# Two expert tables laid side by side: one 8 KB gather per expert instead of two of 4 KB, and weights made in two parts per block

## The chip, the cores and the metric

One NeuronCore of one Trainium2 chip runs the whole program. The metric is the device time of that core in microseconds (us); the time before is the median of three runs, and everything else is read from one profiled execution of the same kernel.

## What is computed

The reference is one inference step of a two-layer network over 384 tokens of width 1024 (128 context tokens and 256 noisy ones), float32 throughout. Layer 0 mixes the tokens with an RG-LRU, layer 1 with gated linear attention (GLA); after each mixer comes a PEER channel mixer, which is where the change lies. Its core, from the reference:

```python
cand = (v1[..., :, None] + v2[..., None, :]).reshape(T, PEER_HEADS, -1)
sc, pos = lax.top_k(cand, PEER_TOPK)
eid = jnp.take_along_axis(cid, pos, axis=-1)
gate = jax.nn.softmax(sc, axis=-1)
...
ub = jnp.take(u_tab, eb, axis=0)
act = jax.nn.gelu(jnp.einsum('td,thkd->thk', xb, ub).astype(jnp.float32))
vb = jnp.take(v_tab, eb, axis=0)
return jnp.einsum('thk,thkd->td', (gb * act).astype(vb.dtype), vb)
```

So each token picks 16 experts for each of 8 heads. For every expert a row u of 1024 floats (4 KB) is dotted with the token, the result goes through a gelu and is multiplied by the gate, and the row v of the same expert (another 4 KB) is added to the token's output with that weight. Each table has 16,384 rows a layer. 384 x 8 x 16 experts at 8 KB are 402.7 MB a layer.

## The kernel before

The tokens lie in three tiles of 128 (one token to a partition). A **block** is one head of one tile: 24 blocks a layer (`NB`), in the order of `h, t = divmod(b, NT)`, 16 experts (`TOPK`) each, and n numbers the experts through both layers. Each expert of a block is one indirect gather of 128 rows, one row to a partition.

There is no scheduler: every engine runs its own list of instructions, and semaphores join them. Ring buffers set how far one may run ahead of another.

- **GpSimd (POOL)**, `gathers` (lines 302 to 323): for each block it waits for the indices (`idx_ready`), issues the 16 u gathers (L314) into a ring of `US` = 8 buffers, then the 16 v gathers (L321) into a ring of `VS` = 16. A u buffer is free when VectorE has dotted it (`u_free`), a v buffer when TensorE has used it (`v_free`). The rings are 4 KB slices of `arena`, 24 in all.
- **VectorE (DVE)**, `peer` (lines 1068 to 1109): 16 dot products (L1085, in place, `accum_out` keeps the sum), the inner polynomial of the gelu (L1089 to L1091), softmax and dot folded into `ex` (L1095 to L1098), the top 16 of the keys' scores for two blocks ahead (`row_tops`, L1101), the weights (L1105) once ScalarE has the tanh, and then the choice of the experts for two blocks ahead (`choose`, which ends with `idx_ready` at L1053).
- **ScalarE (ACT)**, `peer` (lines 416 to 476): when a head begins it first copies the queries (L421, waits for TensorE), then the tanh (L458), then for each expert a 128 x 128 diagonal matrix of the weights (L467, a ring of `DS` = 8); ahead of expert 8 of a head's first block it copies the scores (L430).
- **TensorE (PE)**, `peer` (lines 714 to 728): for each expert two matmuls (L725) of the diagonal with the two halves of the v row, summed in PSUM; each is two passes in the records, so 4 records an expert. A head's first block begins with the next head's queries (L689), and ahead of expert 8 stand its scores (L698).
- **SyncE (SP)**: streams weights. In PEER it reloads `wq_slab` (1 MB, L264 and L267) for each head when the queries of the one before are done; behind the last one in layer 0 it loads the first four 1 MB slabs of GLA's input weights (`stream`, L257), whose buffers lie idle by then.

In both layers the last block is cut into parts of 8, 4 and 4 experts (`LAST_PARTS`), so that the end of a layer has little left to do; every other block is one part of 16. After layer 0 come the residual and norm, the small projections of GLA, and its large projections, which read the slabs (L651).

```python
mm = pe.matmul(acc[t][:, half * 512:(half + 1) * 512], diag[j % DS][:, :],
               vbuf[n % VS][:, half * 512:(half + 1) * 512], start=False, stop=True,
               skip_group_check=True)
```

Of the kernel before, what the change touches and what calls it, by code (L numbers as in the profile page):

```python
# [17 lines left out]
NT = T // P  # L18
# [5 lines left out]
SLABS = 4  # L24
# [74 lines left out]
def build(nc, x_t, pos_t, vecs, ident_d, mask_d, iota_d, keys_t, ada_w, peer_wq, peer_u, peer_v, rg_w_in,  # L99
          rg_wa, rg_wi, rg_w_out, gla_w_in, w_alpha, state_gla, gla_w_out, y_t, st_rg, st_gla):  # L100
    ctx = ExitStack()
    with ctx:
# [73 lines left out]
        ubuf = [arena[:, i * D:(i + 1) * D] for i in range(US)]  # L176
        vbuf = [arena[:, (US + i) * D:(US + i + 1) * D] for i in range(VS)]
# [53 lines left out]
        def _(sp):  # L231
# [65 lines left out]
        def _(pool):  # L297
# [1051 lines left out]
```

## Time and profile before

| what | value |
|---|---|
| median of 3 runs | 2669.35 us (2669.15 to 2673.39) |
| span of the profiled execution | 2672.5 us |
| TensorE busy, VectorE, ScalarE, GpSimd | 79%, 60%, 19%, 57% |
| software DMA queue (the gathers) | 805.4 MB, 76.4% of 16 engines' span |
| layer 0 PEER, first gather issued to last matmul | 280.64 to 1328.58 us |
| layer 1 PEER, the same | 1616.14 to 2650.42 us |

The profiler gives the profiled execution only as its span, first to last instruction; it is 3.2 us above the median and inside 0.9 us of the slowest of the three runs. The busy shares are means over stages: the two PEER stages make up 2082 us of the span, and the rest (RG-LRU, GLA, head and tail of the program) has other limits and is not touched, but for four slab loads. A profile row names the line, the engine, the operation and the buffers; idle time stands before an instruction with what ended it.

### The profile page before, as it was taken

The numbers are of one execution on the slowest core, as the hardware profiler recorded it, in microseconds if no ns is written. First come the engines' busy times: TensorE is split into PE (matmuls) and PEld (weight loads), VectorE is DVE, ScalarE is ACT, GpSimd is POOL, SyncE is SP. The second block draws the span as 40 slices with busy tenths as digits, with TensorE's granted clock in tenths as the row PEclk, the third lists the DMA queues.
The fourth block names the chain that finished last, engine by engine and source line by source line (L and its number), as shares of the span: only waits on it lengthen the run. The fifth ranks groups of instructions, "written<-read, shape, count | busy, mean of one in ns | idle before, by whom it ended". The sixth has DMA issues, their size and how long they took to land.

```text
span 2672.5 us, 20762 instructions
## 1 busy us (share of the span) xinstructions
PE 2123.0 (79%) x6324; PEld 1045.4 (39%) x6324; DVE 1597.3 (60%) x3961; ACT 498.2 (19%) x1291; POOL 1528.1 (57%) x1543
## 2 busy tenths in 40 slices
PE   6998678696968685976989996786969687788777
PEld 2555433242424332432447654342424243333333
DVE  3244666757576666767432436667576666767655
ACT  2251211111111111111242112110111111111112
POOL 0000577777777767777500005777777777777773
PEclk9999799898989797988989998898989898989989
DMA  9992699999999999999723117999999999999996
GB/s 295 317 327 95 243 410 407 406 404 405 400 399 407 409 401 399 394 410 409 308 68 95 60 36 262 405 400 409 406 406 404 396 407 409 404 407 394 409 409 242
DMA packets 326365, 913.32 MB, mean 342 GB/s; under 512 B 31952, under 2 KB 128464, under 8 KB 325744
## 3 DMA queue, kind: packets, MB, share of 16 engines
q0 software_dynamic: 221184, 805.40, 76.4%
q1 hardware_dynamic: 97840, 101.20, 11.8%
q10 hardware_dynamic: 7232, 5.39, 0.7%
q8 instruction: 52, 0.85, 0.1%
q14 instruction: 57, 0.47, 0.0%
HBM read 909.26 MB, written 2.63 MB: 341 GB/s over the span
## 4 chain that ended last, share of the span: by engine, by line
PE 22%; POOL 10%; DMA 9%; DVE 4%; issue 4%; ACT 1%; DVEq 0%; ACTq 0%; POOLq 0%
PE psum L725 11%; DMA arena<-in_peer_u,idx 9%; POOL arena L314 7%; PE psum L651 5%; POOL arena L321 3%; PE psum L689 2%; PE psum L827 2%; DVE arena L1085 1%; PE psum L905 1%; PE psum L880 1%; PE psum L638 0%; PE psum L809 0%; ACT diag L467 0%; DVE i12u L1020 0%; ACT arena L377 0%
## 5 line engine op out<-in xcount | busy, mean ns | idle before, releaser
L725 PE MATMUL psum<-arena,diag 128*128 128x512 f32 x3072 | 1413.2, 622 | 464.7 <-ACT diag L467 464.5
L1085 DVE SCALAR_TENSOR_TENSOR arena<-arena,xtok 128x1024 f32<-128x1024 f32 x768 | 939.6, 1225 | 639.7 <-DMA arena<-in_peer_u,idx 611.2
L314 POOL DMA_INDIRECT arena<-in_peer_u,idx x768 | 778.9, 1014 | 874.1 <-issue 523.3
L725 PEld LDWEIGHTS psum<-arena,diag 128*128 128x128 f32 x3072 | 608.5, 200 | 1257.4 <-issue 1257.4
L321 POOL DMA_INDIRECT arena<-in_peer_v,idx x768 | 745.2, 970 | 234.2 <-issue 211.6
L467 ACT ACTIVATE diag<-ident,wts 128x128 f32<-128x128 f32 x768 | 259.3, 393 | 475.1 <-PE psum L725 370.0
L651 PE MATMUL psum<-arena,slab 128*128 128x384 f32 x672 | 227.7, 497 | 7.3 <-DVE arena L1154 5.1
L689 PE MATMUL psum<-area 128*128 128x384 f32 (+1 forms) x512 | 165.2, 482 | 8.3 <-DMA area<-in_peer_wq 8.3
L651 PEld LDWEIGHTS psum<-arena,slab 128*128 128x128 f32 x672 | 128.2, 193 | 101.3 <-issue 13.0
L458 ACT ACTIVATE tanh<-inner 128x16 f32<-128x16 f32 (+2 forms) x52 | 11.1, 213 | 760.7 <-DVE inner L1091 760.7
L689 PEld LDWEIGHTS psum<-area 128*128 128x128 f32 x512 | 99.0, 194 | 76.0 <-DMA area<-in_peer_wq 10.9
L421 ACT ACTIVATE area<-psum 128x384 f32<-128x384 f32 (+1 forms) x32 | 15.3, 477 | 314.8 <-PE psum L689 314.8
L616 PE MATMUL psum<-slab,cond 128*2 128x256 f32 x528 | 53.1, 409 | 21.3 <-DMA slab<-in_ada_w 21.3
L1085 DVE DVE_READ_ACCUMULATOR arena<-arena,xtok 128x1 f32 x768 | 63.0, 82 | 0.0
L827 PE MATMUL psum<-slab,arena 128*128 128x256 f32 x192 | 41.6, 379 | 0.0
L362 ACT ACTIVATE arena<-xT 128x384 f32<-128x384 f32 x40 | 20.1, 520 | 101.8 <-DVE xT L1163 46.7
L1196 DVE COPY arena<-psum 128x256 f32<-128x256 f32 x12 | 5.1, 424 | 56.1 <-PE psum L827 56.1
L827 PEld LDWEIGHTS psum<-slab,arena 128*128 128x128 f32 x192 | 36.5, 190 | 5.2
L616 PEld LDWEIGHTS psum<-slab,cond 128*2 128x2 f32 x528 | 19.2, 89 | 47.9 <-DMA slab<-in_ada_w 27.9
L1045 DVE TENSOR_TENSOR small<-ab,iota 128x512 f32<-128x512 f32 x48 | 35.7, 743 | 0.0
L1048 DVE TENSOR_TENSOR small<-small,i 128x512 f32<-128x512 f32 x48 | 33.2, 692 | 1.7
L1049 DVE TENSOR_REDUCE e<-small 128x32 f32<-128x512 f32 x48 | 32.9, 686 | 1.6
(218 smaller groups left out, 1329.1 us busy)
## 6 DMA issues: line engine op xcount, KB each, us to landing
slab<-in_ada_w SPq DMA_DIRECT2D x33, 1024.0 KB, 8.3
area<-in_peer_wq SPq DMA_DIRECT2D x16, 1024.0 KB, 16.4
arena<-in_peer_u,idx POOLq DMA_INDIRECT x768, 8.1
arena<-in_peer_v,idx POOLq DMA_INDIRECT x768, 7.9
slab<-in_gla_w_in SPq DMA_DIRECT2D x12, 1024.0 KB, 5.6
keys<-in_ada_w SPq DMA_DIRECT2D x8, 1024.0 KB, 9.1
area<-in_ada_w SPq DMA_DIRECT2D x7, 1024.0 KB, 7.9
slab<-in_rg_w_in SPq DMA_DIRECT2D x5, 1024.0 KB, 11.7
```

Source lines behind the costliest of these rows:

```text
L314: pool.indirect_dma_start(ubuf[n % US], None, u_rows, bass.IndirectOffsetOnAxis(ap=rows[:, j:j + 1], axis=0)).then_inc(u_in[n % US], 16)
L321: pool.indirect_dma_start(vbuf[n % VS], None, v_rows, bass.IndirectOffsetOnAxis(ap=rows[:, j:j + 1], axis=0)).then_inc(v_in[n % VS], 16)
L467: act.activation(diag[j % DS][:, :], ident[:, :], ACT.Copy, scale=wts[t][:, j:j + 1]).then_inc(sem("diag_ready"), 1)
L616: mm = pe.matmul(out[32 * s:32 * s + 2, o:o + SW], cond[:, c, :], slab[SLOT[k]][:, c, :], start=False, stop=(c == C - 1), skip_group_check ...
L651: mm = pe.matmul(out, slab[SLOT[k]][:, c, (n % 2) * P:(n % 2 + 1) * P], rhs[:, c, :], start=(c == 0), stop=(c == C - 1))
L689: mm = pe.matmul(bank[6 + half][:, t0 * P:T], wq_slab[:, c, half * P:(half + 1) * P], hP[:, c, t0 * P:T], start=(c == 0), stop=(c == C - 1))
L725: mm = pe.matmul(acc[t][:, half * 512:(half + 1) * 512], diag[j % DS][:, :], vbuf[n % VS][:, half * 512:(half + 1) * 512], start=False, st ...
L827: mm = pe.matmul(bank[(2 + i) % 4][:, 0:SW], hT[:, c, t * P:(t + 1) * P], slab[SLOT[k]][:, c, :], start=(c == 0), stop=(c == C - 1))
L1045: link(dve.tensor_tensor(oh, ab[:, :, :].unsqueeze(3).to_broadcast([P, 2, TOPK, TOPK]), iota16[:, :].unsqueeze(1).unsqueeze(1).to_broadcas ...
L1048: link(dve.tensor_tensor(oh, oh, i12[:, :, :].unsqueeze(2).to_broadcast([P, 2, TOPK, TOPK]), ALU.mult))
L1049: link(dve.tensor_reduce(e12[:, :, :], oh, AX_X, ALU.add))
L1085: dve.scalar_tensor_tensor(ubuf[n % US], ubuf[n % US], 1.0, xtok[:, t * D:(t + 1) * D], ALU.mult, ALU.mult, accum_out=dots[t][:, j:j + 1]) ...
```

## The change

On the host the tables u and v are joined along their last axis, so one table `peer_uv` has rows of 8 KB with u in front. One gather brings an expert's whole row into one of `RS` = 16 buffers of 8 KB. Twelve of them lie in `arena`, four are the weight slabs; so SP may load GLA's first slabs only when the last row of layer 0 is used (a new wait). The dots are written into the first half of the row, TensorE reads the second half, and the buffer is free when TensorE has used it. Every block but the last is cut into two parts of 8 experts, each with its own inner, tanh and weights; `row_tops` stays in the first part, `choose` behind the last.

```diff
-US, VS, DS = 8, 16, 8
+RS, DS = 16, 8
+PARTS = (range(0, 8), range(8, 16))
...
-NSTEP = NB - 1 + len(LAST_PARTS)
+NSTEP = 2 * (NB - 1) + len(LAST_PARTS)
...
-        ubuf = [arena[:, i * D:(i + 1) * D] for i in range(US)]
-        vbuf = [arena[:, (US + i) * D:(US + i + 1) * D] for i in range(VS)]
+        row = [arena[:, 2 * i * D:2 * (i + 1) * D] for i in range(RS - SLABS)]
+        row += [s[:, :, :].rearrange("p c n -> p (c n)") for s in slab[0:SLABS]]
...
-            return LAST_PARTS if b == NB - 1 else (range(TOPK),)
+            return LAST_PARTS if b == NB - 1 else PARTS
...
             sp.dma_start(st_rg, rgfin[:, :, :]).then_inc(sem("st_rg_out"), 16)
+            sp.wait_ge(row_free, NB * TOPK)
             stream(PLACE["gla_in", 0], len(SEQ))
...
-                    for part in parts(b):
-                        for j in part:
-                            n = (layer * NB + b) * TOPK + j
-                            if n >= US:
-                                pool.wait_ge(u_free, n - US + 1)
-                            pool.indirect_dma_start(
-                                ubuf[n % US], None, u_rows,
-                                bass.IndirectOffsetOnAxis(ap=rows[:, j:j + 1], axis=0)).then_inc(u_in[n % US], 16)
-                        for j in part:
-                            n = (layer * NB + b) * TOPK + j
-                            if n >= VS:
-                                pool.wait_ge(v_free, n - VS + 1)
-                            pool.indirect_dma_start(
-                                vbuf[n % VS], None, v_rows,
-                                bass.IndirectOffsetOnAxis(ap=rows[:, j:j + 1], axis=0)).then_inc(v_in[n % VS], 16)
+                    for j in range(TOPK):
+                        n = (layer * NB + b) * TOPK + j
+                        if n >= RS:
+                            pool.wait_ge(row_free, n - RS + 1)
+                        pool.indirect_dma_start(
+                            row[n % RS], None, rows_of,
+                            bass.IndirectOffsetOnAxis(ap=rows[:, j:j + 1], axis=0)).then_inc(row_in[n % RS], 16)
...
-                                           vbuf[n % VS][:, half * 512:(half + 1) * 512], start=False, stop=True,
+                                           row[n % RS][:, D + half * 512:D + (half + 1) * 512], start=False, stop=True,
...
-                            dve.wait_ge(u_in[n % US], 16 * (n // US + 1))
-                            dve.scalar_tensor_tensor(ubuf[n % US], ubuf[n % US], 1.0, xtok[:, t * D:(t + 1) * D],
+                            dve.wait_ge(row_in[n % RS], 16 * (n // RS + 1))
+                            dve.scalar_tensor_tensor(row[n % RS][:, 0:D], row[n % RS][:, 0:D], 1.0,
+                                                     xtok[:, t * D:(t + 1) * D],
...
-                        if ahead < NB:
+                        if ahead < NB and i == 0:
                             dve.wait_ge(sem("s_ev"), 2 * (PH * layer + ahead // NT + 1))
                             row_tops(ahead)
...
-                        if layer * NB + b >= 3:
-                            dve.wait_ge(v_free, (layer * NB + b - 2) * TOPK)
+                        if i == 0 and layer * NB + b >= 3:
+                            dve.wait_ge(row_free, (layer * NB + b - 2) * TOPK)
...
-        "ada_w": a["ada_w"], "peer_wq": a["peer_wq"], "peer_u": a["peer_u"], "peer_v": a["peer_v"],
+        "ada_w": a["ada_w"], "peer_wq": a["peer_wq"],
+        "peer_uv": np.concatenate([a["peer_u"], a["peer_v"]], axis=2),
```

## Rows read from the trace of the kernel before

**Rows 1.** Page of the profile: span, busy time by engine, DMA rate in 40 slices.

```profile
span 2672.5 us, 20762 instructions
...
PE 2123.0 (79%) x6324; PEld 1045.4 (39%) x6324; DVE 1597.3 (60%) x3961; ACT 498.2 (19%) x1291; POOL 1528.1 (57%) x1543
...
GB/s 295 317 327 95 243 410 407 406 404 405 400 399 407 409 401 399 394 410 409 308 68 95 60 36 262 405 400 409 406 406 404 396 407 409 404 407 394 409 409 242
```

**Rows 2.** Chain that ended last, share of the span by line.

```profile
PE psum L725 11%; DMA arena<-in_peer_u,idx 9%; POOL arena L314 7%; PE psum L651 5%; POOL arena L321 3%; PE psum L689 2%; PE psum L827 2%; DVE arena L1085 1%; PE psum L905 1%; PE psum L880 1%; PE psum L638 0%; PE psum L809 0%; ACT diag L467 0%; DVE i12u L1020 0%; ACT arena L377 0%
```

**Rows 3.** Stretches in PEER: busy us (x instructions) by engine, PE clock, DMA share, GB/s.

```profile
360.00:380.00 20.00, 11.38 (x23) 5.12 (x24) 13.26 (x51) 4.67 (x14) 15.22 (x16) 0.74 1.03 410
1620.00:1640.00 20.00, 14.23 (x40) 7.73 (x39) 16.30 (x51) 3.23 (x8) 10.20 (x10) 0.74 0.84 292
1660.00:2620.00 960.00, 748.90 (x1756) 339.27 (x1756) 642.98 (x1649) 148.90 (x465) 717.35 (x730) 0.90 1.02 405
```

**Rows 4.** Page: software DMA queue; issues of the u gathers with median landing time.

```profile
q0 software_dynamic: 221184, 805.40, 76.4%
...
arena<-in_peer_u,idx POOLq DMA_INDIRECT x768, 8.1
```

**Rows 5.** Stretches ahead of PEER, where weights arrive; columns as in rows 3.

```profile
80.00:120.00 40.00, 37.96 (x222) 19.87 (x217) 9.39 (x16) 9.58 (x20) 0.00 (x0) 1.00 1.04 332
160.00:200.00 40.00, 38.62 (x226) 20.84 (x224) 18.46 (x23) 12.71 (x19) 0.00 (x0) 1.00 1.06 338
```

**Rows 6.** Timeline of POOL, both layers: start, duration, [idle before].

```profile
280.64 1.08 POOL L314 DMA_INDIRECT arena<-in_peer_u,idx  x1 [276.11 <-DVE flag L1053]
...
1616.14 0.94 POOL L314 DMA_INDIRECT arena<-in_peer_u,idx  x1 [301.05 <-issue]
...
1636.35 1.97 POOL L314 DMA_INDIRECT arena<-in_peer_u,idx  x1 [0.30 <-issue]
```

**Rows 7.** Timeline, the last four experts of each layer.

```profile
1319.78 8.80 PE L725 MATMUL psum<-arena,diag 128*128 128x512 f32 x16 [3.13 <-ACT diag L467]
...
2635.79 1.12 POOL L321 DMA_INDIRECT arena<-in_peer_v,idx  x1 [0.30 <-issue]
...
2638.72 1.22 DVE L1085 SCALAR_TENSOR_TENSOR arena<-arena,xtok 128x1024 f32<-128x1024 f32 x1
...
2641.62 8.80 PE L725 MATMUL psum<-arena,diag 128*128 128x512 f32 x16 [3.13 <-ACT diag L467]
```

**Rows 8.** Timeline of one block: DVE, then PE.

```profile
701.82 0.17 DVE L1089 TENSOR_TENSOR inner<-dots 128x16 f32<-128x16 f32 x1
...
705.47 0.17 DVE L1105 SCALAR_TENSOR_TENSOR wts<-tanh,ex 128x16 f32<-128x16 f32 x1
...
711.54 0.06 DVE L1053 MEMSET flag<- 128x1 f32 x1
...
720.03 1.50 PE L698 MATMUL psum<-keys,area 128*128 128x128 f32 x12
...
722.49 13.97 PE L725 MATMUL psum<-arena,diag 128*128 128x512 f32 x32 [0.96 <-ACT diag L467]
```

**Rows 9.** Chain in order of time: queries of one head on PE.

```profile
2028.62 10.34 PE psum L689 x32
```

**Rows 10.** Stretches of 2 us around an idle time of PE; columns as in rows 3.

```profile
1260.00:1262.00 2.00, 0.00 (x0) 0.00 (x0) 1.93 (x5) 0.00 (x0) 1.39 (x3) 0.50 1.02 406
1266.00:1268.00 2.00, 2.00 (x3) 0.67 (x2) 0.00 (x0) 0.40 (x1) 1.39 (x3) 0.50 1.06 418
1270.00:1272.00 2.00, 2.00 (x6) 0.90 (x5) 0.00 (x0) 0.40 (x1) 1.39 (x3) 1.00 1.03 412
```

**Rows 11.** Page: the dot products of DVE.

```profile
L1085 DVE SCALAR_TENSOR_TENSOR arena<-arena,xtok 128x1024 f32<-128x1024 f32 x768 | 939.6, 1225 | 639.7 <-DMA arena<-in_peer_u,idx 611.2
```

**Rows 12.** Timeline: SP's four slabs for GLA, and PE's first matmuls on them.

```profile
961.21 38.66 SPq L257 DMA_DIRECT2D slab<-in_gla_w_in  x4
...
1362.55 2.29 PE L651 MATMUL psum<-arena,slab 128*128 128x384 f32 x3
```

More of the change, by code:

```diff
@@ L96, in __call__, with build @@
         self.need(self.mark(ins))
-def build(nc, x_t, pos_t, vecs, ident_d, mask_d, iota_d, keys_t, ada_w, peer_wq, peer_u, peer_v, rg_w_in,
+def build(nc, x_t, pos_t, vecs, ident_d, mask_d, iota_d, keys_t, ada_w, peer_wq, peer_uv, rg_w_in,
           rg_wa, rg_wi, rg_w_out, gla_w_in, w_alpha, state_gla, gla_w_out, y_t, st_rg, st_gla):
@@ L212, in build @@
         slab_in = [sem(f"slab_in{i}") for i in range(SLABS + 2)]
-        u_in = [sem(f"u_in{i}") for i in range(US)]
-        v_in = [sem(f"v_in{i}") for i in range(VS)]
-        u_free, v_free = sem("u_free"), sem("v_free")
+        row_in = [sem(f"row_in{i}") for i in range(RS)]
+        u_used, row_free = sem("u_used"), sem("row_free")
         (vec_in, const_in, x_in, pos_in, bd_in, gla_small_in, mask_in, s0_in) = (
@@ L302, in gathers @@
             def gathers(layer):
-                u_rows = peer_u.rearrange("l n d -> (l n) d")
-                v_rows = peer_v.rearrange("l n d -> (l n) d")
+                rows_of = peer_uv.rearrange("l n d -> (l n) d")
                 pool.wait_ge(sem("h_ready"), 32 * (layer + 1))
@@ L439, in total @@
                 def total(t):
-                    act.wait_ge(v_free, (layer * NB + NB - NT + t + 1) * TOPK)
+                    act.wait_ge(row_free, (layer * NB + NB - NT + t + 1) * TOPK)
                     act.activation(xtok[:, t * D:(t + 1) * D], acc[t], ACT.Copy).then_inc(sem("acc_ev"), 1)
@@ L456, in peer @@
                         p = slice(part[0], part[-1] + 1)
-                        act.wait_ge(sem("inner_ready"), layer * NSTEP + b + i + 1)
+                        act.wait_ge(sem("inner_ready"), layer * NSTEP + 2 * b + i + 1)
                         act.activation(tanh[t][:, p], inner[t][:, p], ACT.Tanh, scale=GELU_C
                                        ).then_inc(sem("tanh_ready"), 1)
-                        act.wait_ge(sem("w_ready"), layer * NSTEP + b + i + 1)
+                        act.wait_ge(sem("w_ready"), layer * NSTEP + 2 * b + i + 1)
                         for j in part:
@@ L465, in peer @@
                             if n >= DS:
-                                act.wait_ge(v_free, n - DS + 1)
+                                act.wait_ge(row_free, n - DS + 1)
                             act.activation(diag[j % DS][:, :], ident[:, :], ACT.Copy,
@@ L721, in peer @@
                         n = (layer * NB + b) * TOPK + j
-                        pe.wait_ge(v_in[n % VS], 16 * (n // VS + 1))
+                        pe.wait_ge(row_in[n % RS], 16 * (n // RS + 1))
                         pe.wait_ge(sem("diag_ready"), n + 1)
@@ L725, in peer @@
                             mm = pe.matmul(acc[t][:, half * 512:(half + 1) * 512], diag[j % DS][:, :],
-                                           vbuf[n % VS][:, half * 512:(half + 1) * 512], start=False, stop=True,
+                                           row[n % RS][:, D + half * 512:D + (half + 1) * 512], start=False, stop=True,
                                            skip_group_check=True)
-                        mm.then_inc(v_free, 1)
+                        mm.then_inc(row_free, 1)
                 pe.wait_ge(sem("acc_ev"), NT * (layer + 1))
@@ L1050, in choose @@
                 if b >= 4:
-                    dve.wait_ge(v_free, (layer * NB + b - 3) * TOPK)
+                    dve.wait_ge(row_free, (layer * NB + b - 3) * TOPK)
                 link(dve.scalar_tensor_tensor(idx[q][:, :], e12[:, 0, :], float(NK), e12[:, 1, :], ALU.mult, ALU.add))
@@ L1083, in peer @@
                             n = (layer * NB + b) * TOPK + j
-                            dve.wait_ge(u_in[n % US], 16 * (n // US + 1))
-                            dve.scalar_tensor_tensor(ubuf[n % US], ubuf[n % US], 1.0, xtok[:, t * D:(t + 1) * D],
+                            dve.wait_ge(row_in[n % RS], 16 * (n // RS + 1))
+                            dve.scalar_tensor_tensor(row[n % RS][:, 0:D], row[n % RS][:, 0:D], 1.0,
+                                                     xtok[:, t * D:(t + 1) * D],
                                                      ALU.mult, ALU.mult, accum_out=dots[t][:, j:j + 1]
-                                                     ).then_inc(u_free, 1)
-                        dve.wait_ge(u_free, (layer * NB + b) * TOPK + part[-1] + 1)
+                                                     ).then_inc(u_used, 1)
+                        dve.wait_ge(u_used, (layer * NB + b) * TOPK + part[-1] + 1)
                         link(dve.tensor_tensor(inner[t][:, p], dots[t][:, p], dots[t][:, p], ALU.mult))
@@ L1098, in peer @@
                         link(dve.tensor_tensor(ex[q][:, p], ex[q][:, p], dots[t][:, p], ALU.mult))
-                        if ahead < NB:
+                        if ahead < NB and i == 0:
                             dve.wait_ge(sem("s_ev"), 2 * (PH * layer + ahead // NT + 1))
                             row_tops(ahead)
-                        dve.wait_ge(sem("tanh_ready"), layer * NSTEP + b + i + 1)
-                        if layer * NB + b >= 3:
-                            dve.wait_ge(v_free, (layer * NB + b - 2) * TOPK)
+                        dve.wait_ge(sem("tanh_ready"), layer * NSTEP + 2 * b + i + 1)
+                        if i == 0 and layer * NB + b >= 3:
+                            dve.wait_ge(row_free, (layer * NB + b - 2) * TOPK)
                         dve.scalar_tensor_tensor(wts[t][:, p], tanh[t][:, p], 1.0, ex[q][:, p], ALU.add, ALU.mult
```

## Prediction

> **What bounds the kernel now.** I began with the page: no engine is busy throughout (PE 79%, DVE 60%), but in 28 of the 40 slices the transfer rate stands at 394 to 410 GB/s [rows 1]. The chain that ended last agrees: it wanders between the u gathers' DMA, POOL issuing them and PE's L725 [rows 2], which is what a ring looks like when a transfer is at its bottom. Then the stretches. In the quiet middle of PEER the 16 DMA engines are full (share 1.03) and move 410 GB/s, and the best slices of the page have 409 and 410 [rows 1, 3]; I take 409.5; over 960 us of layer 1 the mean is 405; only at a layer's start is it low, 292 GB/s in 20 us [rows 3]. A u gather lands 8.1 us after its issue, although it needs only 1.28 us of the engines (0.524 MB at 409.5 GB/s), so several stand in the queue [rows 4]: in PEER the kernel waits for DMA throughput, not for latency or for an engine.
>
> The two PEER stages, from first gather issued to last matmul, take 1047.9 us (280.64 to 1328.58) and 1034.3 us (1616.14 to 2650.42) [rows 6, 7]. The change can win only there.
>
> **Part 1: bigger packets.** The bytes stay: 384 gathers of 8 KB rows replace 768 of 4 KB ones a layer. What can change is the cost of a packet. Ahead of PEER, where weights arrive in 1 KB runs, the engines are just as full (share 1.04 and 1.06) but move 332 and 338 GB/s [rows 5]. With 16 engines a 1 KB packet at 335 takes 48.9 ns, a 4 KB packet at 409.5 takes 160.0 ns. The line through both has 0.03617 ns per byte and 11.9 ns per packet. So an 8 KB packet is estimated at 160.0 + 4096 x 0.03617 = 308.1 ns instead of 320.0, and a gather (8 packets per engine) at 2.465 us instead of 2 x 1.280 = 2.560 (425 GB/s). No gather with 8 KB rows is in the trace, so the price is bounded: 2.560 if a row is cut into two packets or the packet cost is none of this kind; 2.370 if the packet cost vanished altogether. I take 2.465, since it extends two measured points by one doubling. Over 768 gathers the step from 2.560 to 2.465 is worth 73 us.
>
> The Trainium skill ("DMA: Bandwidth & Descriptors", section "Why small descriptors are slow (HBM only)") puts the fixed cost at about 3 cycles a packet beside 128 beats for 4 KB; by that the saving would be about 1.1%, some 23 us instead of 73, and the result near 2608. The rows' 11.9 ns of 160.0 speak for more than that.
>
> **Part 2: the layer's start.** Today POOL issues 8 u gathers and then stands until DVE, still choosing the experts of block 1, frees a buffer; then each issue lasts 1.97 us instead of 0.94 while DVE's dots run back to back, plus 0.30 between them [rows 6]. That is the hole of 292 GB/s [rows 3]: (409.5 - 292)/409.5 x 20 = 5.7 us in those 20 us, about 9 in all with the 20 after. With 16 rows of 1 MB the queue holds 16 x 2.465 = 39 us of work at once. At that ring's first turn I expect a short gap, because block 0's first row can't be freed before PE has done the queries of head 1, whose weights now share the engines with a full queue: I put it at 3 us, beside 2 us from issue to full rate.
>
> **Part 3: the wait on SP.** The four GLA slabs, now issued at 961.2 us into the full queue [rows 12], move behind layer 0. A 1 MB weight load costs 64 x 48.9 ns = 3.13 us of the engines, so PEER of layer 0 loses 12.5 us of transfers. Behind the last row they need about 13 us; PE reads the first 34 us after its last L725 (1328.6 to 1362.55) [rows 7, 12]. Nothing else is queued on SP but the later slabs, which follow one another at once. Cost 0; if the cover were gone it would be at most 13 us.
>
> **Part 4: the layer's end.** Today the last v row lands at about 2641, and PE runs its last four experts from 2641.62 for 8.80 us: 9.1 us behind the landing [rows 7]. Now u arrives with v, so behind the last landing come a dot, the inner steps, tanh and weights: 2.90 us from the start of the last dot (2638.72) to PE, then 8.80. The end is 11.7 us behind the landing, 2.6 more a layer.
>
> **Part 5: instructions.** 384 gathers fewer on POOL a layer: it is not the bound, and is hidden by DMA now. Two parts add to 23 blocks three inner steps, one `ex` and one `wts` on DVE (0.17 us each [rows 8]) and one tanh: DVE's block is 16 x 1.23 for the dots [rows 11], 3.65 for inner, tops and weights (701.82 to 705.47), 6.1 for `choose` (to 711.54) [rows 8], plus 1.2: 31 us under 39.4 of DMA. Hidden, and if not, under 1 us a block.
>
> **The sum** for layer 1: 2 + 3 + 384 x 2.465 (946.6) + 7 weight loads x 3.13 (21.9) + 11.7 = 985.2, against 1034.3: 49.1 won. Layer 0 loses the slabs too and should take the same 985.2, against 1047.9: 62.7. Together 111.8 us from 2672.5 in the profiled execution; that lies 3.2 above the median, so the forecast is 2669.35 - 111.8 = 2557.5, **about 2558 us**. (A check of the method: for layer 1 before it gives 2 + 983.0 + 21.9 + 9.1 = 1016; the missing 18 us are the 9 of the start and 9 of slices under 409.)
>
> **What comes next: PE and the ring.** A row's buffer is now held until PE is done with it, through the landing of the 7 rows behind it. PE needs 13.97 us for 8 experts at full clock, 1.50 for scores [rows 8], 10.34 for queries [rows 9]. After an idle stretch the granted clock is 0.50 (1.2 GHz), and it stayed there some 6 us into the next work before it was 1.00 (2.4 GHz) [rows 10]; that costs 3 us a part. A head is 6 x 13.97 + 11.8 + 6 x 3 = 114 us of PE in 3 x 39.4 + 3.1 = 121 of DMA: it fits, but barely. The tight spot is a head's first block. If the block before lands at 0, PE starts its last part at 3, ends at 20 (cold), queries until 30.4, ACT copies them only then and makes the tanh that stood behind, PE frees the new block's first row at about 34, and the gather for it can start at 36. The queue runs dry at 39.4 to 42.5. Margin 3 to 6 us.
>
> **The rivals.**
> - **Cut packets, 2630 us.** The 8 KB row moves as two 4 KB packets, or costs as much. Each layer is 2 + 3 + 983.0 + 21.9 + 11.7 = 1021.6: 12.7 and 26.3 won, 39 in all. For it: no packet of this queue above 4 KB is in the trace, so nothing shows that it makes them. Against it: nothing in the trace either. The Trainium skill (same page, section "SWDGE vs HWDGE vs iDMA") says a packet of the software path is preferably at most 4096 B, which would give this case; no row here shows it.
> - **PE late at each head, slower: about 2716 us.** If the clock stays low through the queries (10.34 more) and 3 us longer in each of the two parts beside them, PE is 16.3 us late. Less the margin of 5, that is 11.3 us in 14 heads, 158 us on 2558. It decides from about 13 us a head. Against it: queries now follow directly behind 8 experts, so PE is at work before them; today at 2028.62 they took 10.34, full clock.
> - **POOL becomes the bound, slower: near 3100.** If POOL's time for a gather grows with its bytes, it is 2 x 1.97 + 0.30 = 4.24 us beside back-to-back dots, for half of the rows, against 2.24 for the others: mean 3.24 x 384 = 1244 a layer. Against it: the number of rows, 128, stays.
> - **No saving of any kind, 2669:** the new holds eat what the start and slabs give.
> - **Packets free of cost, 2485:** 2.370 a gather, 73 us less than forecast.
>
> **Chances.** Forecast 0.58, cut packets 0.25, PE late 0.06, POOL 0.03, no saving 0.04, free packets 0.04. The likeliest case alone reaches from 2535 (2.435 a gather) to 2608 (2.53); with the second case and 12 us for a gap at each turn the range is 2525 to 2650, which leaves out 0.17. About 0.2% is what a measurement of this kernel can tell from no change. Faster by more than that: 0.58 + 0.25 + 0.04 and part of the doubtful cases, 0.89; within 0.03; slower 0.08.
>
> **What would show it.** DMA rate in the middle of PEER at 420 to 428 GB/s (410: cut packets, and twice the packets per gather). No hole in the first 40 us. POOL busy about halved, at 0.94 to 1.1 us a gather. Layers of about 985 us. L651 not waiting for a slab. PE's share up, with queries still at 10.3. Wrong if the DMA share falls below 1.0 at the first block of each head, or POOL's mean is near 2 us.

## The result and the profile after

| | median | runs |
|---|---|---|
| before | 2671.37 us | 2669.15 to 2674.18, 4 runs |
| after | 2607.26 us | 2606.61 to 2611.63, 4 runs |

The ratio is 0.9765 with an interval of 0.9751 to 0.9778: 64 us are won (2671.37 - 2607.26), where the prediction said 112. The direction is the one forecast, and 2607 is inside the range of 2525 to 2650; what is to be explained is the 47 us that are missing.

The page of the kernel after, its lines that answer to [rows 1, 2, 4]: span, busy time, rate in 40 slices, two DMA queues, the chain by line, two groups of instructions, and two landing times.

```profile
span 2604.7 us, 20351 instructions
...
PE 2125.3 (82%) x6324; PEld 1044.5 (40%) x6324; DVE 1598.7 (61%) x4191; ACT 486.4 (19%) x1337; POOL 948.2 (36%) x775
...
GB/s 303 318 328 112 276 406 419 420 418 421 417 417 418 410 418 412 408 420 419 268 73 98 61 37 294 421 418 421 418 421 418 421 418 413 418 409 415 417 421 184
...
q0 software_dynamic: 110592, 805.36, 74.7%
q1 hardware_dynamic: 97840, 101.20, 12.1%
...
DMA slab<-in_peer_uv,idx 28%; PE psum L717 24%; PE psum L643 8%; DMA arena<-in_peer_uv,idx 8%; POOL slab L313 3%; POOL arena L313 2%; DMA slab<-in_ada_w 2%; DMA area<-in_peer_wq 2%; PE psum L681 2%; PE psum L819 2%; PE psum L608 2%; DVE slab L1077 2%; PE psum L897 1%; PE psum L758 1%; ACT diag L459 1%
...
L717 PE MATMUL psum<-arena,diag 128*128 128x512 f32 x2304 | 1087.6, 632 | 368.6 <-ACT diag L459 368.6
L313 POOL DMA_INDIRECT arena<-in_peer_uv,idx x576 | 698.9, 1213 | 1530.7 <-PE psum L717 879.6
...
area<-in_peer_wq SPq DMA_DIRECT2D x16, 1024.0 KB, 25.4
...
arena<-in_peer_uv,idx POOLq DMA_INDIRECT x576, 17.1
```

POOL fell from 57% to 36%. The rate in PEER's slices went from 394 to 410 up to 408 to 421, not to 425. The gathers' queue has 110,592 packets for the same 805 MB, half of the 221,184 in [rows 4], so a row of 8 KB does go as one packet (98,304 of the packets are rows; the other 12,288 are 16 of 4 B for each gather). The chain is now landings of rows (28% + 8%) and PE's L717. POOL stands 879.6 us behind PE's L717, which is only the ring being full.

Stretches of the kernel after; columns as in [rows 3]. The last line is the kernel before, in the same 20 us of layer 0.

```profile
300.00:320.00 20.00, 9.24 (x22) 5.27 (x23) 7.88 (x30) 0.49 (x1) 1.66 (x1) 0.62 1.02 418
324.00:326.00 2.00, 0.90 (x2) 0.49 (x3) 1.65 (x4) 1.70 (x7) 0.00 (x0) 1.00 0.45 113
340.00:360.00 20.00, 16.68 (x42) 7.36 (x41) 16.26 (x47) 6.10 (x21) 10.67 (x9) 1.00 1.01 423
1240.00:1260.00 20.00, 16.35 (x33) 6.82 (x33) 10.92 (x23) 3.43 (x11) 8.76 (x8) 0.84 1.01 421
1268.00:1270.00 2.00, 2.00 (x6) 0.95 (x5) 1.25 (x3) 1.28 (x4) 0.00 (x0) 1.00 0.26 107
1270.00:1272.00 2.00, 2.00 (x6) 0.81 (x5) 1.23 (x2) 0.00 (x0) 0.00 (x0) 1.00 0.07 29
1640.00:2560.00 920.00, 738.91 (x1712) 331.46 (x1711) 641.71 (x1751) 139.36 (x476) 438.43 (x360) 0.92 1.01 418
...
300.00:320.00 20.00, 11.88 (x32) 6.49 (x30) 14.42 (x26) 0.98 (x2) 16.45 (x12) 0.84 0.83 263
```

In the quiet middle the engines are full and move 421 to 423 GB/s, over 920 us 418. The hole at the layer's start is gone (418 in 300:320, against 263 before), and a short one at 324 to 330 took its place. At the layer's end (1268 on) the share drops to 0.07, about one engine of 16, while rows still land.

DVE's dot products, each with its idle time and what ended it; the first is row 32 of layer 0, the last is row 384.

```profile
371.96 1.25 DVE L1077 SCALAR_TENSOR_TENSOR slab<-slab,xtok 128x1024 f32<-128x1024 f32 x1 [1.25 <-DMA slab<-in_peer_uv,idx]
...
1240.80 1.23 DVE L1077 SCALAR_TENSOR_TENSOR arena<-arena,xtok 128x1024 f32<-128x1024 f32 x1 [1.25 <-DMA arena<-in_peer_uv,idx]
...
1243.29 1.22 DVE L1077 SCALAR_TENSOR_TENSOR arena<-arena,xtok 128x1024 f32<-128x1024 f32 x1 [1.25 <-DMA arena<-in_peer_uv,idx]
...
1245.78 1.23 DVE L1077 SCALAR_TENSOR_TENSOR arena<-arena,xtok 128x1024 f32<-128x1024 f32 x1 [1.26 <-DMA arena<-in_peer_uv,idx]
...
1275.53 1.23 DVE L1077 SCALAR_TENSOR_TENSOR slab<-slab,xtok 128x1024 f32<-128x1024 f32 x1 [1.22 <-DMA slab<-in_peer_uv,idx]
```

In the middle each dot waits 1.25 us for its row, and they begin 2.49 us apart: the starts of the dots show when the rows land. Layer 0's PEER went from 1047.9 us to 1010.5 (first gather issued at 278.75, last matmul ended at 1282.25 + 7.03 = 1289.28), layer 1's from 1034.3 to 1006.8. The sum had 985.2 for both, so 25.3 and 21.6 us of the 47 are here.

### The profile page after: what moved, and what is told of

Its sections match the earlier page's. It is cut to its first block, busy times and chain, and to the rows that moved or that the text cites. A ratio compares the mean times of both kernels' runs of the same rounds, so it can differ in the third digit from the quotient of the medians.

```text
span 2604.7 us, 20351 instructions
## 1 busy us (share of the span) xinstructions
PE 2125.3 (82%) x6324; PEld 1044.5 (40%) x6324; DVE 1598.7 (61%) x4191; ACT 486.4 (19%) x1337; POOL 948.2 (36%) x775
## 3 DMA queue, kind: packets, MB, share of 16 engines
q0 software_dynamic: 110592, 805.36, 74.7%
q1 hardware_dynamic: 97840, 101.20, 12.1%
## 4 chain that ended last, share of the span: by engine, by line
PE 42%; DMA 41%; DVE 6%; POOL 5%; issue 3%; ACT 2%; SPq 0%; DVEq 0%; ACTq 0%
DMA slab<-in_peer_uv,idx 28%; PE psum L717 24%; PE psum L643 8%; DMA arena<-in_peer_uv,idx 8%; POOL slab L313 3%; POOL arena L313 2%; DMA slab<-in_ada_w 2%; DMA area<-in_peer_wq 2%; PE psum L681 2%; PE psum L819 2%; PE psum L608 2%; DVE slab L1077 2%; PE psum L897 1%; PE psum L758 1%; ACT diag L459 1%
## 5 line engine op out<-in xcount | busy, mean ns | idle before, releaser
L717 PE MATMUL psum<-arena,diag 128*128 128x512 f32 x2304 | 1087.6, 632 | 368.6 <-ACT diag L459 368.6
L313 POOL DMA_INDIRECT arena<-in_peer_uv,idx x576 | 698.9, 1213 | 1530.7 <-PE psum L717 879.6
L717 PEld LDWEIGHTS psum<-arena,diag 128*128 128x128 f32 x2304 | 459.9, 203 | 984.4 <-issue 984.4
L1077 DVE SCALAR_TENSOR_TENSOR arena<-arena,xtok 128x1024 f32<-128x1024 f32 x576 | 687.0, 1223 | 268.4 <-DMA arena<-in_peer_uv,idx 262.7
L1077 DVE SCALAR_TENSOR_TENSOR slab<-slab,xtok 128x1024 f32<-128x1024 f32 x192 | 235.4, 1228 | 227.4 <-DMA slab<-in_peer_uv,idx 227.4
L717 PE MATMUL psum<-slab,diag 128*128 128x512 f32 x768 | 337.4, 593 | 0.0
L313 POOL DMA_INDIRECT slab<-in_peer_uv,idx x192 | 245.3, 1278 | 71.5 <-issue 39.3
L459 ACT ACTIVATE diag<-ident,wts 128x128 f32<-128x128 f32 x768 | 235.0, 389 | 107.8 <-DVE wts L1098 107.4
L643 PE MATMUL psum<-arena,slab 128*128 128x384 f32 x672 | 227.8, 497 | 7.1 <-DVE arena L1147 4.9
L450 ACT ACTIVATE tanh<-inner 128x8 f32<-128x8 f32 (+1 forms) x98 | 20.3, 207 | 1140.5 <-DVE inner L1084 1140.5
L717 PEld LDWEIGHTS psum<-slab,diag 128*128 128x128 f32 x768 | 146.2, 190 | 183.4 <-issue 183.4
L681 PE MATMUL psum<-area 128*128 128x384 f32 (+1 forms) x512 | 165.6, 483 | 35.0 <-DMA area<-in_peer_wq 35.0
L643 PEld LDWEIGHTS psum<-arena,slab 128*128 128x128 f32 x672 | 128.6, 194 | 100.7 <-issue 12.8
L681 PEld LDWEIGHTS psum<-area 128*128 128x128 f32 x512 | 99.4, 195 | 102.7 <-DMA area<-in_peer_wq 37.7
L1098 DVE SCALAR_TENSOR_TENSOR wts<-tanh,ex 128x8 f32<-128x8 f32 (+1 forms) x98 | 16.4, 167 | 81.6 <-issue 52.6
## 6 DMA issues: line engine op xcount, KB each, us to landing
area<-in_peer_wq SPq DMA_DIRECT2D x16, 1024.0 KB, 25.4
slab<-in_rg_w_in SPq DMA_DIRECT2D x5, 1024.0 KB, 11.7
```

The costliest lines, as they stand in the source:

```text
L313: pool.indirect_dma_start(row[n % RS], None, rows_of, bass.IndirectOffsetOnAxis(ap=rows[:, j:j + 1], axis=0)).then_inc(row_in[n % RS], 16)
L450: act.activation(tanh[t][:, p], inner[t][:, p], ACT.Tanh, scale=GELU_C).then_inc(sem("tanh_ready"), 1)
L459: act.activation(diag[j % DS][:, :], ident[:, :], ACT.Copy, scale=wts[t][:, j:j + 1]).then_inc(sem("diag_ready"), 1)
L643: mm = pe.matmul(out, slab[SLOT[k]][:, c, (n % 2) * P:(n % 2 + 1) * P], rhs[:, c, :], start=(c == 0), stop=(c == C - 1))
L681: mm = pe.matmul(bank[6 + half][:, t0 * P:T], wq_slab[:, c, half * P:(half + 1) * P], hP[:, c, t0 * P:T], start=(c == 0), stop=(c == C - 1))
L1077: dve.scalar_tensor_tensor(row[n % RS][:, 0:D], row[n % RS][:, 0:D], 1.0, xtok[:, t * D:(t + 1) * D], ALU.mult, ALU.mult, accum_out=dots[t ...
```

## The experiments

All times are medians beside runs of the kernel before on the same chip; those medians were 2669.9 to 2672.5.

**E1: the same ring and parts, but two gathers of 4 KB a row.**

```diff
-pool.indirect_dma_start(row[n % RS], None, rows_of, ...).then_inc(row_in[n % RS], 16)
+for k, table in enumerate((peer_u, peer_v)):
+    pool.indirect_dma_start(row[n % RS][:, k * D:(k + 1) * D], None, table.rearrange("l n d -> (l n) d"),
+                            ...).then_inc(row_in[n % RS], 16)
-dve.wait_ge(row_in[n % RS], 16 * (n // RS + 1))
+dve.wait_ge(row_in[n % RS], 32 * (n // RS + 1))
```

> The changed kernel (2607 us) with each row fetched by two gathers of 4 KB from the two old tables into the two halves of the same buffer: ring, parts and slab wait as changed, only packet size and number of gathers as before. If the saving per packet is what pays (2.49 us a row after, 2.56 before), the time rises by 768 x 0.07 = 54 us to about 2661, the rate in the middle of PEER falls to 409 to 410 GB/s at a DMA share of 1.03. If ring, start and slabs give all of the gain, it stays at 2607. If POOL can't issue two gathers a row in the time (2 x 1.24 us alone, up to 2 x 2.27 beside the dots), it goes above 2680 with a DMA share under 1.

Measured: 2749.25 us (2745.02 to 2751.57), ratio 1.0297 (1.0280 to 1.0314). The chain from the page, and the stretch 1680 to 2680:

```profile
POOL arena L313 23%; PE psum L717 17%; POOL slab L313 9%; PE psum L643 7%; DMA slab<-in_peer_v,idx 7%; DMA arena<-in_peer_v,idx 3%; PE psum L681 3%; DMA slab<-in_ada_w 2%; PE psum L608 2%; PE psum L819 2%; DVE slab L1077 1%; DMA area<-in_peer_wq 1%; PE psum L897 1%; PE psum L758 1%; ACT diag L459 1%
...
1680.00:2680.00 1000.00, 769.41 (x1730) 343.54 (x1731) 648.28 (x1771) 141.39 (x482) 780.22 (x721) 0.89 1.00 385
```

POOL's own instructions are now 32% of the chain, and the rate is 385 over a thousand microseconds. An issue takes 0.94 us, but up to 1.99 beside DVE's dots, plus 0.30 between two: in the thousand microseconds that is 780 + 721 x 0.30 = 996 us of POOL, so with two gathers a row POOL is the limit. So the packet's price can't be read here, and another thing can: without the joined table, this ring and these parts are 3% slower than the kernel before. In the kernel before, a u issue took 1014 ns in the mean and a v issue 970; here they take 1107 and 1057 (buffers in `arena`). POOL was near its limit there too: 717 + 730 x 0.30 = 936 of 960 us [rows 3].

**E2: the kernel before, with the slab loads behind the last row.**

```diff
+            sp.wait_ge(v_free, NB * TOPK)
             stream(PLACE["gla_in", 0], len(SEQ))
```

> The kernel before with only the new wait of SP ahead of GLA's first slabs. If the 4 MB they bring are 4 x 3.13 us of full DMA engines in PEER and free behind it, the time falls by 12.5 us to about 2659. If the transfers were hidden already, or if the slabs come late for L651, it stays at 2671 or rises by up to 13 us.

Measured: 2658.63 us (2655.29 to 2662.00), ratio 0.9955 (0.9938 to 0.9972): 11.8 us less. In the trace PEER of layer 0 takes 1035.6 us instead of 1047.9, and layer 1's first gather comes 285.4 us behind its end, where it was 287.6. Part 3 stands: 4 MB of weights out of the full queue are worth 12 us and cost nothing behind it.

**E3: E2 with a u ring of 16, eight of its buffers in the slabs.**

```diff
-US, VS, DS = 8, 16, 8
+US, VS, DS = 16, 16, 8
-        ubuf = [arena[:, i * D:(i + 1) * D] for i in range(US)]
+        ubuf = [arena[:, i * D:(i + 1) * D] for i in range(8)]
+        ubuf += [s[:, 4 * k:4 * k + 4, :].rearrange("p c n -> p (c n)") for s in slab[0:SLABS] for k in range(2)]
```

> The kernel before with that wait and a u ring of 16 buffers of 4 KB (8 of them in the slabs), still two gathers of 4 KB. If the hole at each layer's start came from the u ring of 8, 9 us a layer go beside the 12.5 of the slabs: 2671 - 12.5 - 18 = about 2641. If the start is limited otherwise (POOL at 2.27 us a gather beside the dots), it equals the run with the wait alone, 2659.

Measured: 2649.38 us (2648.51 to 2654.06), ratio 0.9930 (0.9914 to 0.9947): 9.3 less than E2, half of the 18. Layer 1 begins at another time in each run, so the stretches are those from 4 us behind its first gather: E2 (first gather at 1600.04), then E3 (1596.03).

```profile
1604.00:1624.00 20.00, 18.04 (x42) 9.22 (x41) 15.69 (x49) 3.24 (x8) 10.12 (x8) 0.66 0.80 275
...
1600.00:1620.00 20.00, 17.16 (x41) 8.71 (x40) 15.68 (x49) 3.23 (x8) 16.03 (x14) 0.66 1.00 368
1620.00:1640.00 20.00, 12.31 (x30) 6.18 (x29) 19.51 (x61) 3.64 (x11) 16.34 (x13) 0.83 0.98 355
```

The deeper ring takes about half of the start's hole. What is left is POOL's issue at its slower pace: 16.03 + 14 x 0.30 fill the first 20 us, and two gathers a row keep that.

**E4: the kernel after, dots over 128 of 1024 columns.** It leaves out 7/8 of each dot product, so its output is another one.

```diff
-dve.scalar_tensor_tensor(row[n % RS][:, 0:D], row[n % RS][:, 0:D], 1.0, xtok[:, t * D:(t + 1) * D], ...
+dve.scalar_tensor_tensor(row[n % RS][:, 0:P], row[n % RS][:, 0:P], 1.0, xtok[:, t * D:t * D + P], ...
```

> The changed kernel with dots over 128 of the 1024 columns; it leaves out 7/8 of each dot product, so the weights are other numbers. DVE's time for a row falls from 1.23 to about 0.2 us. If the DMA engines alone set 2.49 us a row, the rate in the middle stays 421 GB/s and the time falls by only 2 to 4 us (the last dots). If DVE's dots beside POOL's descriptors or the SBUF traffic of the dots slow the transfers, the rate rises to 425 or more and the time falls by 8 us or more.

Measured: 2603.71 us (2603.43 to 2603.96), ratio 0.9754 (0.9737 to 0.9770): 3.5 less than the kernel after. Its stretch of 920 us:

```profile
1640.00:2560.00 920.00, 745.65 (x1706) 333.21 (x1705) 310.01 (x1749) 139.81 (x477) 338.88 (x357) 0.91 1.01 417
```

DVE's work is halved (310 us against 642) and the rate is the same: neither DVE nor POOL beside it holds up the kernel after. What is left is DMA, whose engines are full (share 1.01). The 3.5 us are within what was said for the dots that stand on the path at both ends of a layer.

**E5: E1 and E4 together**, which differs from E4 by the packet's size and the number of gathers alone (it leaves out the same 7/8 of the dots).

> Two gathers of 4 KB a row into the same ring, and dots over 128 of the 1024 columns (7/8 of each dot product is left out), so that DVE no longer stretches POOL's gathers: POOL then needs 2 x 1.24 = 2.49 us a row, less than 2.56. If a 4 KB packet itself costs more, the rate in the middle is 409 to 410 GB/s at a DMA share of 1.03 and the time is 2604 + 768 x 0.07 = about 2658. If packet size is worth nothing and the 2749 us of the two gathers with full dots was POOL alone, the rate is 421 and the time about 2604 to 2610.

Measured: 2657.41 us (2654.72 to 2658.86), ratio 0.9945 (0.9930 to 0.9960). Its dots, and its stretch of 920 us:

```profile
1710.32 0.29 DVE L1077 SCALAR_TENSOR_TENSOR arena<-arena,xtok 128x128 f32<-128x128 f32 x1 [2.22 <-DMA arena<-in_peer_v,idx]
...
1712.88 0.29 DVE L1077 SCALAR_TENSOR_TENSOR arena<-arena,xtok 128x128 f32<-128x128 f32 x1 [2.26 <-DMA arena<-in_peer_v,idx]
...
1640.00:2560.00 920.00, 732.60 (x1684) 328.91 (x1684) 311.23 (x1731) 136.02 (x465) 664.67 (x699) 0.91 1.03 407
```

With the short dots POOL has time over, if little (665 + 699 x 0.30 = 874 of 920 us), the engines are full at share 1.03, and rows land 2.56 us apart. The difference to E4, 53.7 us over 768 rows, is 0.070 us a row: the price of 16 packets of 4 KB and two gathers against 8 of 8 KB and one, on each engine. Part 1 had 0.095 (73 us). The medians of before beside E4 and E5 differ by 0.5 us.

**E6: the kernel after, weights laid on the host so that a slab is one 8 KB run a partition.**

```diff
-src = peer_wq[layer].rearrange("(c p) n -> p c n", p=P)
-sp.dma_start(wq_slab, src[:, :, 0:SW]).then_inc(wq_in, 16)
+src = peer_wq[layer]
+sp.dma_start(wq_slab, src[0]).then_inc(wq_in, 16)
...
+    def slabs(w):
+        return w.reshape(w.shape[0], C, P, -1, SW).transpose(0, 3, 2, 1, 4)
```

> The changed kernel with all weight slabs laid on the host so that each slab is one run of 8 KB a partition instead of eight of 1 KB; same bytes, same order. If a packet costs 11 to 12 ns beside its bytes, a 1 MB slab takes 2.49 us of full engines instead of 3.13: 14 loads in PEER give 9 us, and of the 57 ahead of layer 0's PEER (36 us of engine time) the part on the chain, 10 to 25 us: 2570 to 2590 in all, with the rate ahead of PEER above 380 GB/s where the engines are full. If the size of the packet matters only on the gathers' software queue, it stays at 2607 and 332 to 338 GB/s.

Measured: 2593.68 us (2592.14 to 2597.71), ratio 0.9708 (0.9693 to 0.9723): 13.6 less than the kernel after, and outside the 2570 to 2590 expected. Page lines, and a stretch ahead of PEER:

```profile
q1 hardware_dynamic: 15408, 101.20, 10.1%
...
area<-in_peer_wq SPq DMA_DIRECT2D x16, 1024.0 KB, 9.3
...
80.00:120.00 40.00, 38.98 (x265) 21.09 (x254) 11.44 (x20) 8.75 (x19) 0.00 (x0) 1.00 0.89 340
```

Packets of the weights' queue fell from 97,840 to 15,408, and `wq_slab` lands 9.3 us after its issue, not 25.4. In the trace the two PEER stages are 6.4 and 3.0 us shorter (1004.1 and 1003.8), the 9 us expected of the 14 loads. The missing part is the one ahead of PEER: the rate per full share rose (340 at 0.89 is 382; in [rows 5] it is 319), but the engines now stand idle for a tenth of that time, and the first gather is issued at 280.80, no sooner than the 278.75 of the kernel after. Ahead of PEER the engines were not what the time hung on.

**E7: the kernel after, last block in four parts of 4.**

```diff
-LAST_PARTS = (range(0, 8), range(8, 12), range(12, 16))
+LAST_PARTS = (range(0, 4), range(4, 8), range(8, 12), range(12, 16))
```

> The changed kernel with the last block of each layer in four parts of 4. If PE's 16 experts in one go (30.4 us from the weights of the first 8) set the end of a layer, PE begins 10 us earlier and the end is set by the last landing: 3 us a layer less, about 2601. If the last landing sets it already, it stays at 2607.

Measured: 2603.93 us (2599.52 to 2605.04), ratio 0.9745 (0.9731 to 0.9758), 3.3 less than the kernel after; the two intervals overlap. The last dot of layer 0 and PE behind it, then PE at the end of layer 1:

```profile
1278.29 1.23 DVE L1077 SCALAR_TENSOR_TENSOR slab<-slab,xtok 128x1024 f32<-128x1024 f32 x1 [1.23 <-DMA slab<-in_peer_uv,idx]
...
1281.20 7.11 PE L717 MATMUL psum<-slab,diag 128*128 128x512 f32 x16 [2.74 <-ACT diag L459]
...
2573.51 8.59 PE L717 MATMUL psum<-slab,diag 128*128 128x512 f32 x16 [3.01 <-ACT diag L459]
```

PE had done all earlier experts and stood 2.74 us when the last weights came: the end is 10.0 us behind the last dot's start (1288.31 - 1278.29), against 13.75 in the kernel after. In layer 1 PE was done too and stood 3.01 us, but its last four experts took 8.59 us instead of 7.03: the end is 11.5 us behind the last dot's start (2570.59), against 12.8. The mechanism is shown in both layers, the size is at the edge of what can be told.

**E8: the kernel after with one part of 16.**

```diff
-PARTS = (range(0, 8), range(8, 16))
+PARTS = (range(16),)
```

> The changed kernel with one part of 16 a block in the same ring of 16. By the ring's theory no buffer comes free before all 16 rows have landed: weights 5.3 us behind the last landing, PE's first expert 3.4 us at the low clock, 4 to 5 us from the next issue to its landing, so a block takes 37 + 14 = 51 us instead of 40 and the time is about 3060. If two parts were of no use, it stays at 2607.

Measured: 3216.51 us, one run; 1.20 of before. One block boundary on PE and POOL, and a stretch of it:

```profile
715.64 6.62 PE L717 MATMUL psum<-arena,diag 128*128 128x512 f32 x8 [23.83 <-ACT diag L459]
...
720.17 0.94 POOL L313 DMA_INDIRECT arena<-in_peer_uv,idx  x1 [26.76 <-PE psum L717]
...
716.00:720.00 4.00, 4.00 (x5) 1.46 (x5) 3.79 (x14) 1.95 (x7) 0.00 (x0) 0.50 0.00 0
```

Weights come only behind the 16th dot, all 16 buffers are held by then, and the queue is empty (share 0.00) until PE has used the first. It cost 156 us more than said. Part of that is to be seen here: PE, idle for 23.83 us, ran its first experts at clock 0.50, and POOL's first reissue came 4.5 us after PE began (720.17 - 715.64). The two parts are no refinement; a ring of one block can't do without them.

**E9: the kernel after with 14 rows in the ring.**

```diff
-RS, DS = 16, 8
+RS, DS = 14, 8
```

> The changed kernel with a ring of 14 rows (12 in the arena, 2 in slabs). Two rows less are 5 us less between a row's landing and the moment the queue runs dry. By the prediction's margin of 3 to 6 us at each head's first block the queue would now run dry for 0 to 2 us 14 times and a little in other blocks: 2607 to 2640. If the margin is in truth wider than 5 us everywhere, the time stays at 2607; if it is used up already, it rises by 5 us at every block, to about 2800.

Measured: 2617.81 us (2616.41 to 2618.85), ratio 0.9796 (0.9781 to 0.9811): 10.6 more than the kernel after. Its stretch of 920 us:

```profile
1640.00:2560.00 920.00, 743.02 (x1716) 332.69 (x1714) 642.60 (x1756) 139.71 (x475) 435.34 (x360) 0.91 1.01 415
```

415 against 418 GB/s. Two rows fewer are 5 us less of queue. Where they are lost is seen from the 22nd row of layer 0, just past the ring's first turn, in the kernel after and in E9:

```profile
347.09 1.22 DVE L1077 SCALAR_TENSOR_TENSOR arena<-arena,xtok 128x1024 f32<-128x1024 f32 x1 [0.80 <-DMA arena<-in_peer_uv,idx]
...
352.38 1.23 DVE L1077 SCALAR_TENSOR_TENSOR arena<-arena,xtok 128x1024 f32<-128x1024 f32 x1 [1.25 <-DMA arena<-in_peer_uv,idx]
```

Counted from the first gather (278.75 and 279.21) that row is 4.8 us later in E9, and the last row of the layer 5.3; in layer 1 it is 5.6 and 7.9. So most of the loss is at the two starts, where there is no margin at all, and behind them, the heads and all else, it is 0.5 us in layer 0 and 2.3 in layer 1. At the heads the margin of 16 rows was thus 5 us or more nearly everywhere: the upper end of the 3 to 6 of the prediction, or beyond it.

**E10: E6 and E7 together.**

> Both edits that gained: weights in 8 KB runs (2594) and the last block in four parts (3 us less): about 2590, 0.7% under the changed kernel, if the two places are independent, as they should be, the one being ahead of PEER and the other at a layer's end.

Measured: 2593.07 us (2591.63 to 2598.15), ratio 0.9708 (0.9694 to 0.9721), the same as E6. So E7's gain doesn't add up visibly. E6 and E10 are the fastest kernels here, 2.9% below before and 0.5% below the change alone.

## Why the prediction was right or wrong

**Right: the direction, and the kind of each step.** An 8 KB row is one packet, transfers stay the bound (E4), slabs move at no cost (E2), POOL is off the path, parts and the new holds fit. By single changes 64 us split up as 11.8 for the slabs (E2) and 53.7 for the packets (E5 less E4). That leaves -1.4 for all else, which is zero within what these runs can tell (each median is good to some 4 us); that a better start and a later end cancel in it is argued, not shown. It is also one order of taking the steps: with full dots and two gathers a row, ring and parts cost time (E1), and the joined table is then worth 142 us. The time by itself would not have told the cases apart, for 2607 is nearer to the 2630 of the cut packets than to 2558; and it is inside the range because of what the sum missed, not by a gather of 2.53 us, with which the prediction reached 2608. The gather took 2.49.

**Wrong: three terms of the sum, and one that it had left out.** Per layer it had 2 + 3 + 946.6 + 21.9 + 11.7. Read from the dots of the kernel after, row by row:

| term | predicted | layer 0 | layer 1 |
|---|---|---|---|
| issue to full rate, and the start's gap | 5 | 7.4 | 6.3 |
| 384 rows | 946.6 | 955.2 | 955.2 |
| 7 weight loads at 3.13 | 21.9 | 21.9 | 21.9 |
| steps inside the layer, in no term | 0 | 12.3 | 10.6 |
| end behind the last dot's start | 11.7 | 13.75 | 12.8 |
| PEER | 985.2 | 1010.5 | 1006.8 |

The rows' term is 384 x 2.4875 (undisturbed dots, 1245.78 - 1240.80 over 2). The weight loads are carried over from the prediction; in E4, where nearly every dot waits for its row, one load delays the rows by 3.11 us (1755.71 - 1735.19 for seven rows, less 7 x 2.4875). The start is what row 32 has above 32 x 2.4875 and two weight loads: 371.96 - 278.75 - 79.6 - 6.26 = 7.4. The steps are what remains.

- **Part 1, the packet cost.** The step that failed was the line through a 1 KB packet of one queue and a 4 KB packet of another, carried on to 8 KB: "0.03617 ns per byte and 11.9 ns per packet". An 8 KB row's packet takes 2.4875/8 = 311 ns, not 308.1, so by the step from 4 to 8 KB the fixed cost is 2 x 160 - 311 = 9 ns (with a share of the 4 B packet that each gather brings an engine as well; half the gathers bring half of these). That is 17 us of the 47 missing in the traces, and 19 by the experiments (73 - 53.7). The Trainium skill's rule ("DMA: Bandwidth & Descriptors", section "Why small descriptors are slow (HBM only)") came out at 2608 for the whole, which is the time measured, but not by its reason: it gave the packets 23 us, and they gave 54.
- **The sum was absolute, and its check was not used.** For layer 1 before, the same method gave 1016 against 1034.3, and the prediction put 9 us of the gap to "slices under 409" and left them out of the sum for after. In the kernel after, 12.3 and 10.6 us are of this kind. Rows don't land late at random. From the last weight load of layer 0 on, the dots keep an even pace but for steps of 0.92 to 1.09 us, at 1024.09, 1087.37, 1167.81 and 1223.41. Two DMA queues carry packets of the kind "instruction": q8 (16 in a layer's PEER, 16 KB each, about 1.1 us of one engine) and q14 (22 and 23, 8 KB, 0.33 us); before there were 16 and 24. The steps go with q14. A packet of it comes ahead of each of the four (at 1022.0, 1085.6, 1160.4 and 1221.0), while the q8 packets at 1070.3 and 1144.3 leave the next dots (1073.84, 1154.45) on pace. E4 shows it best. Its dots around one step, with the q14 line of stretch 646 to 651 (packets, MB, share of 16 engines; that stretch has no q8), and the q8 line of 1272 to 1274 in the kernel after:

```profile
647.55 0.29 DVE L1077 SCALAR_TENSOR_TENSOR arena<-arena,xtok 128x128 f32<-128x128 f32 x1 [2.19 <-DMA arena<-in_peer_uv,idx]
651.01 0.29 DVE L1077 SCALAR_TENSOR_TENSOR arena<-arena,xtok 128x128 f32<-128x128 f32 x1 [3.16 <-DMA arena<-in_peer_uv,idx]
653.49 0.29 DVE L1077 SCALAR_TENSOR_TENSOR slab<-slab,xtok 128x128 f32<-128x128 f32 x1 [2.19 <-DMA slab<-in_peer_uv,idx]
...
q14 instruction: 1, 0.01, 0.4%
...
q8 instruction: 1, 0.02, 3.5%
```

The row at 651.01 comes 3.46 us after the one before, 0.97 late, and the next ones keep that delay. Of the 19 steps of 0.8 to 1.0 us that E4 has away from weight loads, 18 follow a q14 packet and one (353.24) a q8 packet alone. Other packets of both queues delay nothing: the q8 packet at 1272.1 ran while only one engine had rows left, and the last dots stayed 2.45 to 2.47 us apart. A packet that delays no row may have run on an engine that was ahead; the engine isn't recorded. What is not explained is the size, for a q14 packet takes 0.33 us and the step is 0.95. So the instruction queue is the likely cause and not a shown one; no run took its packets away.
- **Part 4, the end.** It had the last four experts start when their weights are there, 2.90 us behind the last dot's start. PE is not free then. Its last 16 experts run without a break from 1258.90 on, the first ones at clock 0.50 (the rows: PE's first twelve and last four of them, a stretch of 2 us, SP's slabs, and PE's first use of a slab):

```profile
1258.90 23.52 PE L717 MATMUL psum<-arena,diag 128*128 128x512 f32 x48 [3.65 <-ACT diag L459]
1282.25 7.03 PE L717 MATMUL psum<-slab,diag 128*128 128x512 f32 x16
...
1260.00:1262.00 2.00, 2.00 (x4) 0.90 (x3) 1.23 (x2) 0.80 (x3) 0.00 (x0) 0.50 0.98 410
...
1289.31 5.55 SPq L257 DMA_DIRECT2D slab<-in_gla_w_in  x4
...
1323.29 2.29 PE L643 MATMUL psum<-arena,slab 128*128 128x384 f32 x3
```

The last four begin at 1282.25, 6.7 us behind the last dot's start (1275.53). The weights of the block's first 8 experts come at once and late, and PE is still paying them off. That is 2.1 and 1.1 us more than predicted; with the last block in fours (E7) the ends are 10.0 and 11.5. The prediction also misread the end of before: the last v row, issued at 2635.79 [rows 7] and 7.9 us under way by that page, landed at about 2643.7 and not 2641, so PE ended 6.7 us behind it and not 9.1. The 11.7 of the sum don't rest on that.
- **Part 2, the start**: the hole went and the short gap came where it was forecast, with its cause: the first reissue waits for PE, PE for the queries, and these for weights in a full queue (first gather, queries, reissue):

```profile
278.75 1.08 POOL L313 DMA_INDIRECT arena<-in_peer_uv,idx  x1 [274.22 <-DVE flag L1045]
...
310.76 12.87 PE L681 MATMUL psum<-area 128*128 128x384 f32 x32 [16.08 <-DMA area<-in_peer_wq]
...
327.83 0.93 POOL L313 DMA_INDIRECT arena<-in_peer_uv,idx  x1 [26.18 <-PE psum L717]
```

It was 1.3 and 2.4 us longer than the 5 predicted, and `wq_slab` took 25.4 us to land instead of 16.4: PE waited 16.08 us for it.
- **Part 3**: SP issues the slabs at 1289.31, and L643 starts at 1323.29 without a wait for one, 34.0 us behind, as said. **Part 5**: hidden (E4).
- **PE and the ring**: it fits, as said. E9 puts the margin at a head's first block at 5 us or more, and finds none at the ring's first turn.
- **Rivals.** Cut packets: refuted by the packet count. The Trainium skill's preference for packets up to 4096 B ("DMA: Bandwidth & Descriptors", section "SWDGE vs HWDGE vs iDMA") didn't cut them here. PE late at each head: no, the queries of the head at 677.93 took 10.48 us at clock 1.00, near the 10.34 of [rows 9], and every L681 up to 1060.8 us lasted 485 to 487 ns. POOL as the bound: not from the bytes of a gather, 0.94 us as before, but it was nearer than thought by another way: before, POOL was taken for 936 of 960 us, and E1 has it as the bound at once when the number of gathers doesn't fall.

## What to carry to other kernels

When a queue is the bound, take the pace from the consumer's waits (here DVE's dots, 2.49 us apart), multiply it out, and look at what the real layer has beyond that; a term missing in the reconstruction of before must be carried into the forecast of after, or both be reconstructed and subtracted. A ring as deep as one block needs its results in parts smaller than the block, or the queue drains at each boundary (E8: 23% over the kernel after). And a better layout pays twice: fewer packets, and fewer issues on the engine that a busy neighbour slows (E1 against the change: 142 us, of which the packets are 54).

## What the runs showed of the hardware

- **The slowest DMA engine sets the landings.** At the end of layer 0 the share falls to 0.26 and then 0.07 (1268 to 1272), about one engine of 16, and the last three rows land 2.44 to 2.47 us apart. Fifteen engines were ahead by 5 to 7 us. So a short dip of the mean rate need not cost anything, and the mean rate at the end misses the tail. Which engine lags wasn't resolved, nor why. The Trainium skill ("DMA: Bandwidth & Descriptors", section "Latency and other measured facts") says that engines 7 and 15 are usually slower with transfers of GpSimd's queue; no run here shows it.
- **GpSimd's gather issue is slowed by VectorE**: 0.94 us alone, 1.97 to 1.99 beside back-to-back dots, at 4 KB and 8 KB rows alike ([rows 6], and the row below from the kernel after). With the dots cut to 128 columns (E4, second row) the mean falls from 1213 to 954 ns. With two gathers a row the slow issue made POOL the limit at 385 GB/s (E1).

```profile
1596.93 1.99 POOL L313 DMA_INDIRECT slab<-in_peer_uv,idx  x1 [0.30 <-issue]
...
L313 POOL DMA_INDIRECT arena<-in_peer_uv,idx x576 | 549.5, 954 | 1668.8 <-PE psum L717 1056.5
```

- **Small packets wait behind large ones**: the weights' 1 KB runs land in 16.4 us beside 4 KB packets, in 25.4 beside 8 KB ones, and in 9.3 when they are 8 KB themselves (E6). The Trainium skill ("DMA: Bandwidth & Descriptors", section "Queues, rings and completion order") has the engines take turns between queues packet by packet, and this agrees: 64 packets of 48.9 ns an engine, each behind one of 160 or of 311 ns, make 13.4 and 23.0 us (estimates), 2 to 3 us under what was measured.
